# A two-layer expert trunk: dots between all the searches, and 112 fetched tokens in the second expert layer

## What is computed

```python
q = (xb @ w_query).reshape(-1, PEER_HEADS, 2, PEER_QHALF)
s = jnp.einsum('thpd,pkd->thpk', q, sub_keys).astype(jnp.float32)
sv, si = lax.top_k(s, PEER_TOPK)
cand = (sv[:, :, 0, :, None] + sv[:, :, 1, None, :]).reshape(-1, PEER_HEADS, PEER_TOPK * PEER_TOPK)
cidx = (si[:, :, 0, :, None] * N_KEYS + si[:, :, 1, None, :]).reshape(-1, PEER_HEADS, PEER_TOPK * PEER_TOPK)
top_s, top_p = lax.top_k(cand, PEER_TOPK)
eidx = jnp.take_along_axis(cidx, top_p, axis=-1)
g = jax.nn.softmax(top_s, axis=-1)
u = u_tab[eidx]
act = jax.nn.gelu(jnp.einsum('thkd,td->thk', u, xb).astype(jnp.float32))
w = (g * act).astype(xb.dtype)
return jnp.einsum('thk,thkd->td', w, v_tab[eidx])
```

## Time and profile before

| | us |
|---|---|
| median of 3 runs | 1724.0 |
| the three runs | 1723.64, 1736.82, 1724.0 |
| the profiled execution, its own time | 1735.56 |
| span of the profile, first to last instruction | 1733.8 |
| busy: PE, PEld, DVE, ACT, POOL | 1654.8, 1528.1, 1090.0, 212.6, 477.7 |
| mean granted TensorE clock | 0.991 |

### The profile page before, as it was taken

One profiled execution on the slowest core, in us unless ns is written; L12 is line 12 of the kernel. 1 busy time (PEld: TensorE's weight loads), 2 busy tenths in 40 slices (PEclk: granted clock), 3 DMA queues, 4 the chain that ended last, 5 costly groups with the idle time before them and its releaser, 6 DMA issues. The chain is left out here.

```text
span 1733.8 us, 33678 instructions
## 1 busy us (share of the span) xinstructions
PE 1654.8 (95%) x12244; PEld 1528.1 (88%) x12244; DVE 1090.0 (63%) x2432; ACT 212.6 (12%) x617; POOL 477.7 (28%) x420
## 2 busy tenths in 40 slices
PE   9999999999999999999899999999899999999998
PEld 7657899988999999888788888988899999989997
DVE  3262269994599898454546414999358989944442
ACT  2241221111110000000003312111111100000000
POOL 0000011343244446333410001033333445533310
PEclk9999999999999999999899999999999999999999
DMA  4213377999999999999974336799999999999984
GB/s 155 87 47 108 128 260 257 354 385 357 353 404 403 360 391 410 409 410 410 409 294 142 134 126 219 227 354 362 375 334 351 393 393 405 402 392 409 409 340 157
DMA packets 149911, 533.85 MB, mean 308 GB/s; under 512 B 17617, under 2 KB 20434, under 8 KB 149842
## 3 DMA queue, kind: packets, MB, share of 16 engines
q1 hardware_dynamic: 89938, 314.90, 48.6%
q0 software_dynamic: 59904, 218.13, 32.5%
HBM read 531.92 MB, written 1.05 MB: 307 GB/s over the span
## 5 line engine op out<-in xcount | busy, mean ns | idle before, releaser
L236 PE MATMUL ps<-big,raw 128*128 128x160 f32 (+2 forms) x5232 | 844.7, 321 | 27.0 <-DMA raw<-in_u 22.4
L236 PEld LDWEIGHTS ps<-big,raw 128*128 128x128 f32 x5232 | 775.9, 190 | 80.9 <-issue 24.0
L1085 PE MATMUL ps<-big,raw 128*128 (+1 forms) x4096 | 601.2, 304 | 21.3 <-DMA raw<-in_v_rows 6.8
L1085 PEld LDWEIGHTS ps<-big,raw 128*128 128x128 f32 x4096 | 564.9, 191 | 48.2 <-issue 45.0
L1128 POOL DMA_INDIRECT big<-in_u_rows,big x208 | 251.4, 1209 | 883.9 <-DVE big L1254 433.6
L1271 DVE SCALAR_TENSOR_TENSOR big<-big 128x1024 f32<-128x1024 f32 x201 | 257.9, 1283 | 200.5 <-PE ps L1085 116.7
L1128 POOL DMA_INDIRECT big<-in_v_rows,big x208 | 226.1, 1087 | 310.6 <-DVE big L1271 257.5
L1254 DVE CUSTOM_DVE_ANT_0 big<-big 128x1024 f32<-128x1024 f32 x208 | 244.2, 1219 | 11.1 <-DMA big<-in_u_rows,big 11.0
L1168 ACT ACTIVATE big<-ps 128x160 f32 x256 | 77.6, 303 | 550.4 <-PE ps L236 514.4
L1202 DVE MAX8 big<-big 128x8 f32<-128x128 f32 (+1 forms) x99 | 33.5, 339 | 104.6 <-ACT big L1137 92.0
L321 ACT ACTIVATE big<-h 128x272 f32<-128x272 f32 (+1 forms) x32 | 12.7, 419 | 621.4 <-DVE h L1345 571.0
(11 more groups left out here) (162 smaller groups left out, 723.5 us busy)
## 6 DMA issues: line engine op xcount, KB each, us to landing
raw<-in_u SPq DMA_DIRECT2D x256, 512.0 KB
raw<-in_v_rows SPq DMA_DIRECT2D x256, 512.0 KB
raw<-in_query SPq DMA_DIRECT2D x32, 512.0 KB, 3.3
raw<-in_lru_w SPq DMA_DIRECT2D x24, 512.0 KB, 4.0
raw<-in_mla_down SPq DMA_DIRECT2D x17, 512.0 KB, 3.3
raw<-in_mla_out SPq DMA_DIRECT2D x8, 512.0 KB, 3.6
big<-in_u_rows,big POOLq DMA_INDIRECT x208
big<-in_v_rows,big POOLq DMA_INDIRECT x208
```

The lines of the kernel that those rows point to most:

```text
L236: mm = pe.matmul(out, self.mem.raw[:, s, c * P:(c + 1) * P], x[:, c, :], start=(c == 0), stop=(c == DC - 1))
L1085: return pe.matmul(accumulator(c), mem.raw[:, s, c * P:(c + 1) * P], act_w[:, i, :], start=start, stop=False, skip_group_check=True)
```

## The change

Layer 1 fetches rows for 112 tokens instead of 96. That gives TD = 144, GG = 7, NG = 18, and a fourth token copy of 16 tokens, as layer 0 has. SCATTER, SPREAD and MID of layer 1 come one turn later (27, 26 and 23, from 26, 25 and 22). The number of groups stays 16. Six dots now stand behind every search but the first, which makes 8 times in layer 0 and 7 in layer 1. In half 0 the rows may not pass the last dot. The first dot on each copy waits until ScalarE has written the copy. `hot` moves to cells that nothing else uses.

```diff
-GATHERED = (112, 96)
+GATHERED = (112, 112)
 LANES, HEADS_ABREAST = 32, 4
 NBUF = 8
-ROWS_PER_FIND, ROWS_AT_SPREAD, ROWS_PER_GROUP, LAST_ROW_TILE = 6, 9, (2, 2), 118
+ROWS_PER_FIND, ROWS_AT_SPREAD, ROWS_PER_GROUP, LAST_ROW_TILE = 6, 9, 2, 118
@@
-    hot, at = take(at, (4, TOPK, TOPK))
     assert at <= LATE * TD
@@
     ident, at = take(at, (P,))
+    hot, at = take(at, (4, TOPK, TOPK))
@@ def dot(n)
                 wait_row(n)
+                if n % TOPK == 0:
+                    dve.wait_ge(reps_out, 2 * copy_of(n) + 2)
@@
                 find(first, min(2, G - first))
-                if first >= GG:
+                if first:
                     n = rows(n, n + ROWS_PER_FIND)
@@
                 for m in range(NG):
-                    n = rows(n, n + ROWS_PER_GROUP[half])
+                    n = rows(n, n + ROWS_PER_GROUP if half else min(n + ROWS_PER_GROUP, ROWS))
```

## The result

Over 20 runs each the changed kernel took 1738.06 us (1729.94 to 1743.28) and the kernel before 1729.32 us (1723.64 to 1740.27). These are medians, with the lowest and the highest run; they lie 8.7 us apart. The ratio (changed kernel over the kernel before) is 1.0039, 95% interval 1.0023 to 1.0054, which is +6.7 us. The forecast was +3.8 us on the profiled execution and 1728 for the median. In a second comparison, beside the experiments, the ratio was 1.0009 (0.9995 to 1.0023), which is no difference clear of noise.

What follows compares the result with a forecast made beforehand. Full transfers, shared by tiles and rows, were taken to bound the kernel wherever rows are under way. Layer 0 -4.4 and layer 1 +8.2 gave +3.8 us: 1739.4 for the profiled execution, 1728 for the median, range 1706 to 1750.

Steps and rivals of the forecast that it cites:

- The limit: Wherever rows are under way, full transfers shared by halves make a tile cost 2.558 us, whatever its width.
- Width of a tile: Layer 1's 144-column tile takes PE 1.94 us (121 ns a record), bounds 1.81 and 2.155; a row then costs 0.62 us.
- Layer 1: All of layer 1, from the fourth copy to the last four tiles: +8.2 us.
- Half 0: Layer 1's first half of the scatter: 17 periods of 5.13 us plus 2.4 hand-over, 102.5 to 89.6 us, -12.9.
- Half 1: Layer 1's second half of the scatter: 103.9 us to 18 x 5.13 = 92.3, -11.6.
- tail: Layer 1 after the scatter, up to the fold: all 76 tiles at 2.558 us, 172.1 to 194.4 us, +22.3.
- Layer 0: All of layer 0: 18 dots moved into the searches cost +7.5 us, its end saves 11.9; together -4.4.
- The end: Layer 0's folds and the twelve tiles behind: wait for rows and lower clock go, -11.9 us, bounds 0 and -13.
- Narrow tiles pay: Rival: PE sets the pace, so layer 1's 256 tiles save 0.215 us each, -55, giving 1665; 10%.
- Idle transfer time fills up: Rival: dots keep DMA full in the searches, layer 1 reaches its first group after 200 us, not 226, giving 1701; 8%.
- The clock falls in layer 1's tail: Rival: PE's waits there lower its clock; 25 of the 76 tiles slow give 1728 + 33 = 1761; 12%.
- Rows late at layer 1's fold: Rival: the stock of buffered rows is below 4, so the fold waits up to 11.9 us, giving 1740; 12%.

Runs made afterwards that it cites:

- narrow v tiles: Changed kernel with layer 1's v products taking 112 of the 144 dense tokens; 1.0016 (0.9995 to 1.0036) to the kernel before, not timed beside the changed one.
- gathered part alone: Changed kernel with 112 gathered tokens in layer 1, but dots only behind searches at and behind GG; 1.0147 (1.0117 to 1.0176) to the kernel before.
- second queue: ScalarE issues tile loads of slots 1 and 3: on the changed kernel 1.0024, on it with 96 tokens 1.0088, on the kernel before 1.0056, all to before.
- later folds: Kernel before with the first folds at tile 120 instead of 112 in both layers; 1.0033 (1.001 to 1.0057) to the kernel before.
- dots alone: Changed kernel, but layer 1 keeps 96 gathered tokens; 1.0024 (1.0005 to 1.0043) to the kernel before, run again 1.0020 (1.0003 to 1.0037).

## Why the prediction held, step by step

**The limit.** Right. "A tile costs 2.558 us whatever its width" is what the narrow v tiles show (2.54 to 2.58), and the tail of layer 1 went from 2.39 to 194.2 / 76 = 2.56 us a tile, as forecast (194.4).

**Width of a tile.** 1.94 us was forecast, 1.98 came: the first 144 records of layer 1 start 124 ns apart (17.8 us from 1077.02), not 121.

**Layer 1.** To the first group 226.2 was forecast, 225.8 and 222.2 measured. Half 0: 89.6, measured 90.1 and 90.6. Half 1: 92.3, measured 93.0 and 94.0. The folds came in long: 3.49 + 1.75 + 28.1 = 33.3 forecast, 35.2 and 34.4 measured. The twelve tiles were right (28.5, from 1687.03 to 1715.49); the three folds took 6.8 us instead of 5.24, since the clock was at 0.69 between 1680 and 1690:

```profile
1680.00:1690.00 10.00, 10.00 (x64) 10.00 (x63) 5.67 (x5) 0.00 (x0) 3.87 (x4) 0.69 1.02 408
```

The fold found its rows, with no wait: the stock of four was enough. The stages of the table hold +8.1 of the +8.2 forecast, and the means give +6.9. By stage, forecast and means: searches +6.6 and +5.6, half 0 -12.9 and -11.8, half 1 -11.6 and -11.6, tail +22.3 and +20.2, fold +3.65 and +4.6. The tail is less because the forecast started from 172.1, the shortest of the three tails before. The two terms outside, +1.0 for the fourth copy and -0.9 for the last four tiles, came as +0.7 and -0.9 in the first pair of profiles.

**Layer 0.** The searches: +7.5 forecast, and the five one-queue profiles with the moved dots and whole rows average 224.6 against 217.2 for the five without them, +7.4. The tail to tile 112: 0 forecast, 0 measured. The end was mis-sized: -11.9 forecast, 43.3 to a mean of 34.0 is -9.3 (34.8 and -8.5 over the five profiles). The wait went; but I had put all of the slow clock on the wait, and part of it stayed without one. The twelve tiles behind the folds still took 29.0 us where 12 x 2.155 = 25.9, and the stretch had clock 0.91. In the means of the whole layer this gives -3.5 instead of -4.4, and that it is so near is luck: the two halves, put at 0, came 1.9 us shorter and made up for most of the 2.6 that the end fell short, and no run shows why.

**The sum.** +3.8 forecast, +3.4 from the stage means of both layers, +4.0 in the span of the first profiles, and +0.4% and +0.1% in the two comparisons of runs. The mechanism is borne out by the experiments; the closeness of the sum is not evidence of its own, since terms of up to 22 us of either sign were added, single ones were off by up to 2.6, and a stage repeats only within 5.

**The rivals.** *Narrow tiles pay* is refuted by the narrow v tiles and by the gathered part alone. *Idle transfer time fills up*: layer 1's searches went from 351 to 364 GB/s, not to 400, and took 225.8 us, not 200; refuted. *The clock falls in layer 1's tail*: it stayed at 0.99 and fell only at the folds behind it. *Rows late at layer 1's fold*: not in the changed kernel, but it is just what the early dots prevent. I had this rival as a drained stock; the experiment shows how near it is: 18 rows fewer in time are 21.45 us of wait.

The Trainium skill (DMA: Bandwidth & Descriptors, Where 436 GB/s comes from) has about 358 GB/s as the limit from HBM. The traces do not agree: the tails after show 409 to 410 GB/s again, so it was right to price the transfers by the trace.

The Trainium skill (TensorE: Matmul & The Clock Gate, HAM oscillation) describes waits for transfers of about 3 to 5 us. The forecast carried this over to waits of 0.6 us, which that example does not cover, and no fall came with them: waits of 0.5 us at a tile left the clock of the narrow kernel's tail at 0.99.

No kernel tried that does the whole computation beats the one before. Two of the theory's own consequences, the larger share by a second queue and the later folds, were tried for that and lost.

## What to carry to other kernels

Where two queues of transfers are full, ask first how they share and what the other stream's bytes cost, and only then what an engine would save: 27 us less work on PE were worth nothing here. As long as there is no more than one row for each tile, and a shared transfer (2.56 us here) is longer than PE's tile, a stretch costs tiles times PE's tile plus rows times (shared transfer less PE's tile). Narrower tiles then make each row dearer, and the trade of columns for rows was nearly even here. And a wait in front of a late fold need not be an error of place: if the transfers' total is what ends last, moving the fold moves the wait.

## What the runs showed of the hardware

The clock falls around the folds even where PE does not wait. In layer 0 of the changed kernel the folds begin right after the last tile and the stretch from 853 to 891 us has 0.91. In layer 1, in the 10 us from the first fold on, the three profiles of before have 1.00, 0.83 and 1.00, and the changed kernel, whose tail before it has a wait at each tile, 0.69 and 0.83. The cause is not settled.

Within one comparison, how long an execution takes goes with the granted clock. Among the 20 runs of the changed kernel the fastest, 1729.94 us, has a mean clock of 0.996, the slowest, 1743.28, has 0.990, and the correlation is -0.85; in the 22, 23 and 29 runs of the kernel before beside the experiments it is -0.50, -0.43 and -0.75. A single profile can be 6 us from the median, as the one of before was (1735.56 against 1729.32), so a gain of that size read from one pair of profiles, as mine for the dots alone, shows nothing.

Between sessions the same kernel differs by more than the change is worth. The kernel before has a median of 1720.93 us beside the first experiments and 1736.83 half an hour later, both recorded on chip 7. The mean clocks are 0.993 and 0.991, which of PE's 1655 busy us is worth about 3 (an estimate); what makes the rest of the 16 us is open. Only ratios of kernels that ran side by side, or stages of one session, can be compared at this size.
